# Combining the two maps of differential attention in parts of 512 keys, and ahead of the new pair's first maximum where two pairs join

## The reference, cut to what matters

```python
def diff_attention(q, k, v, lam, lam_init, g_sub, slopes):
    ...
    for i in range(S // Q_BLOCK):
        q0 = i * Q_BLOCK
        kend = q0 + Q_BLOCK
        s = jnp.einsum('bqhmd,bkhmd->bhmqk', q[:, q0:kend], k[:, :kend]).astype(jnp.float32) * scale
        ...
        s = jnp.where(allowed, s - slopes[:, None, None, None] * dist, NEG)
        p = jax.nn.softmax(s, axis=-1)
        a = p[:, :, 0] - lam * p[:, :, 1]
        outs.append(jnp.einsum('bhqk,bkhe->bqhe', a.astype(v.dtype), v[:, :kend]))
```

## Time and profile before

| | us |
|---|---|
| median of 3 runs | 2730.36 |
| lowest and highest | 2727.61, 2734.29 |
| the profiled execution's own time | 2732.85 |
| its span in the trace | 2730.8 |
| TensorE busy | 2586.2 (95% of the span) |
| VectorE busy | 1153.6 (42%) |
| ScalarE busy | 893.1 (33%) |
| GpSimd busy | 216.4 (8%) |
| share of TensorE in the chain that ended last | 75% |

### The profile page before, as it was taken

One profiled execution on the slowest core, in us unless ns is written; L12 is line 12 of the kernel. 1 busy time (PEld: TensorE's weight loads), 2 busy tenths in 40 slices (PEclk: granted clock), 3 DMA queues, 4 the chain that ended last, 5 costly groups with the idle time before them and its releaser, 6 DMA issues.

```text
span 2730.8 us, 33929 instructions
## 1 busy us (share of the span) xinstructions
PE 2586.2 (95%) x12825; PEld 2117.3 (78%) x12825; DVE 1153.6 (42%) x2309; ACT 893.1 (33%) x1572; POOL 216.4 (8%) x101
## 2 busy tenths in 40 slices
PE   7999999879999999999999999987899999999998
PEld 6778777668788888888878777765788888888886
DVE  5555566645322223223336546665542232232233
ACT  4554444433211212112236544444322121120222
POOL 1111111112000000000211111111110000000001
PEclk9999999999999999999999999999999999999999
DMA  5100010211111111111220000002111111111112
GB/s 174 55 24 24 16 32 24 62 39 45 46 47 46 54 46 46 54 46 52 94 86 24 24 24 24 24 24 68 47 39 54 46 46 54 46 46 54 45 47 77
DMA packets 219019, 131.42 MB, mean 48 GB/s; under 512 B 15222, under 2 KB 214432, under 8 KB 218664
## 3 DMA queue, kind: packets, MB, share of 16 engines
q1 hardware_dynamic: 213208, 114.38, 14.5%
q10 hardware_dynamic: 5712, 15.73, 1.5%
HBM read 117.47 MB, written 12.62 MB: 48 GB/s over the span
## 4 chain that ended last, share of the span: by engine, by line
PE 75%; issue 9%; DVE 8%; ACT 6%; DVEq 2%; DMA 0%; SPq 0%; ACTq 0%; POOL 0%; POOLq 0%
PE ps L1134 67%; DVE probs L912 2%; PE ps L1266 2%; PE ps L1286 2%; ACT probs L638 2%; ACT pt_hi L656 2%; PE ps L1213 1%; PE ps L1288 1%; DVEq L919 1%; DVE pt_lo L963 1%; DVE probs L940 1%; DVE neg_max L927 1%; ACT sink_exp L641 1%; DVE part L823 0%; PE ps L1115 0%
## 5 line engine op out<-in xcount | busy, mean ns | idle before, releaser
L1134 PE MATMUL ps<-wide_hi,w_hi 128*128 128x512 f32 x3016 | 960.1, 400 | 41.2 <-DVE v_parts L833 10.6
L1134 PE MATMUL ps<-wide_lo,w_hi 128*128 128x512 f32 x3016 | 939.7, 393 | 0.0
L1134 PE MATMUL ps<-wide_hi,w_lo 128*128 128x512 f32 x3016 | 937.6, 392 | 0.0
L1134 PEld LDWEIGHTS ps<-wide_hi,w_hi 128*128 128x128 f32 x3016 | 553.7, 190 | 176.7 <-issue 54.9
L1134 PEld LDWEIGHTS ps<-wide_hi,w_lo 128*128 128x128 f32 x3016 | 571.8, 190 | 122.6
L1134 PEld LDWEIGHTS ps<-wide_lo,w_hi 128*128 128x128 f32 x3016 | 571.5, 190 | 122.5
L638 ACT ACTIVATE probs<-probs,neg_max,slope 128x256 f32<-128x256 f32 (+7 forms) x256 | 202.4, 791 | 339.1 <-DVE neg_max L927 275.3
L714 ACT ACTIVATE w_hi<-w_raw 128x1024 fp32r<-128x1024 f32 x112 | 117.8, 1052 | 453.0 <-PE ps L1134 443.5
L963 DVE TENSOR_TENSOR pt_lo<-ps,pt_hi 128x512 fp32r<-128x512 f32 (+3 forms) x216 | 126.6, 586 | 262.1 <-ACT pt_hi L656 261.7
L718 ACT ACTIVATE ring<-ring 128x1024 f32<-128x1024 f32 x64 | 67.8, 1060 | 491.0 <-DVE ring L1069 491.0
L1089 DVE TENSOR_TENSOR xt<-ps,xt 128x1024 f32 x48 | 58.8, 1225 | 387.1 <-PE ps L1134 387.1
(11 more groups left out here) (139 smaller groups left out, 1836.5 us busy)
## 6 DMA issues: line engine op xcount, KB each, us to landing
w_raw<-in_w_up_dram SPq DMA_DIRECT2D x128, 256.0 KB, 3.0
w_raw<-in_w_down_dram SPq DMA_DIRECT2D x128, 256.0 KB, 3.0
w_raw<-in_w_in_dram SPq DMA_DIRECT2D x92, 256.0 KB, 3.3
x_saved<-xt ACTq DMA_DIRECT2D x16, 512.0 KB, 2.6
w_raw<-in_w_out_dram SPq DMA_DIRECT2D x32, 256.0 KB, 3.3
xt<-x_saved SPq DMA_DIRECT2D x16, 512.0 KB, 3.7
o_out<-cum_saved ACTq DMA_DIRECT2D x2, 2048.0 KB, 8.1
out_dram<-rows SPq DMA_DIRECT2D x4, 1024.0 KB, 5.7
```

Source lines behind the costliest of these rows:

```text
L1134: mm = T.matmul(ps[p][:, bass.ts(t, BANK)], w, h[:, bass.ts(t, BANK)], start=(start and n == 0), stop=(stop and n == 2))
```

## The change

The combination of a step is issued in parts of at most 512 keys, each with its own increment of `combined`, and the first half's transposes wait for the first part only; the second half's wait for the second. At the three joins between differential heads of a layer (steps 40, 48, 56), VectorE combines the last step of the old head before it takes the first maximum of the new head; at every other step the order stays. A function gives the count that a part has reached, and `NCOMB` (48) is the number of parts in a layer, where there were 32 increments.

```diff
     PHASE0 = [sum(phases(u) for u in range(t)) for t in range(NT + 1)]
     NPHASE = PHASE0[NT]
+    NCOMB = sum(phases(t) for t in range(FIRST_A * NQ, NT))
+
+    def combined_at(t, part):
+        return PHASE0[t] - PHASE0[FIRST_A * NQ] + part + 1
...
                     V.drain()
-                    V.scalar_tensor_tensor(out=probs[:, (2 * t) % 4, 0:width], in0=probs[:, (2 * t + 1) % 4, 0:width],
-                                           scalar=lam_ratio[:, c:c + 1], in1=probs[:, (2 * t) % 4, 0:width],
-                                           op0=ALU.mult, op1=ALU.add).then_inc(combined, 1)
+                    for k0 in range(0, width, BANK):
+                        k1 = min(width, k0 + BANK)
+                        V.scalar_tensor_tensor(out=probs[:, (2 * t) % 4, k0:k1], in0=probs[:, (2 * t + 1) % 4, k0:k1],
+                                               scalar=lam_ratio[:, c:c + 1], in1=probs[:, (2 * t) % 4, k0:k1],
+                                               op0=ALU.mult, op1=ALU.add).then_inc(combined, 1)
...
                     t = s.step
                     if s.first and t == 2 * NQ:
                         dve.wait_ge(cum_out, 16 * (l + 1))
-                    if s.first and t < NT:
+                    join = t % NQ == 0 and FIRST_A * NQ < t < NT
+                    if s.first and t < NT and not join:
                         biased_max(t, 0)
                     if s.first and t:
                         if ORDER[(t - 1) // NQ][0] == "A":
                             combine(t - 1)
                         else:
                             invert_sums(t - 1)
+                    if s.first and join:
+                        biased_max(t, 0)
...
                     elif ORDER[half.step // NQ][0] == "A":
-                        pe.wait_ge(combined, NQ * AH * l + half.step - NQ * FIRST_A + 1)
+                        pe.wait_ge(combined, NCOMB * l + combined_at(half.step, half.units[0][1] // 4))
```

## The result

The changed kernel takes 2738.9 us (median of 10 runs, 2737.0 to 2746.4), the kernel before in the same series 2733.2 (10 runs). The ratio is 1.0026, with a 95% interval of 1.0016 to 1.0037: slower by some 6 us, which is still within the 0.3% that the prediction called the same. The median lies above the predicted range of 2725 to 2737. The profiled execution took 2739.29 us, 6.4 more than the one before. Of the 7.9 us between the forecast of 2731.0 and the result, 2.8 lie in the kernel before: the forecast started from its median of three runs, 2730.36, and its median of ten is 2733.2. The change itself was forecast at +0.6 us and measured at +5.7.

What follows compares the result with a forecast made beforehand. TensorE, busy 95% of the span, bounds the kernel; its 28.3 us waiting for combinations was the ceiling. Terms of +0.98 us and -0.4 for the clock gave +0.6, so 2731.0 us from 2730.36; range 2725 to 2737.

Steps and rivals of the forecast that it cites:

- The question of which wait ends last: At each touched place, which wait holds TensorE last once its transposes no longer wait; the transposes' 28.3 us was the ceiling.
- the direct prices: A second part adds 0.14 us to VectorE, between 0.08 and 0.30, counting only ahead of a wait of TensorE.
- Join 40: Transposes start 1.27 us earlier, but this is stood out before the dense piece; each join at 40 and 48 costs 0.14.
- join 56: Two joins without a dense piece: the half's copy starts later behind the exponentials, +0.38 us each, +0.76 in all.
- five-block steps: Eight steps combining five blocks: +0.14 us in four, 0 in the third and last heads, sum +0.56.
- GpSimd comes between the parts: Rival: a GpSimd instruction of 2.40 us holds the second part; four such would be 9.6 us, 2741; chance 1%.
- -0.4 for two spells: TensorE's slow spells at step 48, one a layer: -0.2 us taken for each, with -1.5 left to the range.
- new ones to a rival: Rival: six new slow spells, at four joins and two wide steps, 1.5 us each, make 9: 2740; chance 6%.
- the 0.94 to 0.97: Test: the prediction is wrong if the mean clock of the two touched stretches leaves this range.
- The low part's wait on TensorE: TensorE's value products waiting for the half's low part, 27.6 us before: this wait should rise by about 2 us.
- VectorE's busy time: Over the whole kernel, it should rise by 4 to 7 us with 32 more combination instructions.
- the 0.53 kept at the end of the last head: At the last head's end, two places, the transposes' earlier start is kept whole: -1.06 us in all.

Runs made afterwards that it cites:

- e4: The kernel before with only the combination that runs in step 53 in two parts: 2741.6 us, ratio 1.0025.
- e10: As e4, with TensorE turning the identity 20 times while it waits at step 53: 2732.7 us, ratio 0.9992 to the kernel before.
- e3: The changed kernel, but with the combination that runs in step 53 left whole: 2736.8 us, ratio 1.0005 to the kernel before.
- e11: The kernel before with 14 dummy transposes ahead of the real ones at joins 40, 48 and 56: 2728.1 us, ratio 0.9969.

## Why the prediction was wrong

**What held.** The question of which wait ends last was right, and so were the direct prices. Step 37 to 38 took 0.13 us more and step 38 to 39 0.15 (layer 1: 0.13 and 0.13), predicted 0.14 each. Join 40 of layer 0 took 0.11 to 0.13 more, predicted 0.14, and the transposes, L837 and the dense piece each started within 0.02 us of where the working put them, counted from the first value product (375.23); only the standing before the dense piece was 1.27, not 1.45. At join 56 `L660` started right behind the exponentials and the value product came 0.30 later, predicted 0.38. The transposes' wait fell to 15.7, predicted 16.

**The step that failed** is the sentence on five-block steps: "In the third head GpSimd's work holds VectorE beyond it, and in the last TensorE isn't there yet: 0." I had seen that GpSimd ran there and took it as cover for the 0.14. It was the reverse: with a gap between two parts, the waiting GpSimd instruction came in between, and 0 became 1.13 us per layer, with a spell doubled in layer 0 and a new one in layer 1. In the last head, step 61, the same happened (2.92 us instead of 1.14) and the 0 held, as the sentence says, because TensorE comes for it only later: in layer 0 the parts end at 565.80 and the transposes start at 569.66. The mechanism even stands among the rivals, "GpSimd comes between the parts", with 1% and 2741, some 2 us from the result. That nearness is luck: it supposed four holds of 2.40 us, there were four of which two cost 1.13 each, and the clock and the kernel before's higher median made up the rest. It was argued away by one line alone: "No L510 of these stretches starts while a wide combination runs". That is true of the low parts of weights, L510. GpSimd's other instruction in the stretch, L515, was never looked up: at steps 53 and 61 it is queued behind another one, so that it is ready the moment the first part ends. The test was also wrong in kind: what matters isn't whether a GpSimd instruction runs during the whole combination, but whether one is queued then. At step 61 before, the division's record starts inside the whole combination (560.28) and lasts 2.48 us instead of 1.90: it was waiting.

The Trainium skill, "SBUF — State Buffer", section "SBUF: two separate sides", describes the lock as held for one whole instruction by whichever starts first; 2.68 us against 1.04 for the same two parts agrees. What follows for a split, that the port is given away in its middle, I did not draw from it.

**The clock** was the other mis-sized term. I took -0.4 for two spells that might shrink, and left new ones to a rival; measured, the clock took some 3 to 4 us more than before. In the profiled executions the change brought no net relief at the joins: of the four at steps 40 and 48 two carried a spell before (both 48s), and two after (40 and 48 of layer 1), although each standing was shorter. Standing of 1.27 us was followed by one at 1716.19, where the dense piece took 1.05 instead of 0.70; the same 1.27 in layer 0 was not. Of the granted clocks of 0.93 and 0.94 the first lies outside the 0.94 to 0.97 that the prediction asked for.

**The loss, summed:** 2.3 us directly at step 53, about 1 for the parts and joins as predicted, and some 2 to 3 by the clock, make the 5.7. The last is the remainder; the lost clock of the timed runs puts it at 2.7 to 4.4 (57.5 less 54.8 to 53.1). e4 and e10 show that step 53 alone can bring this much and more, but e3 loses as much clock without it, so where the change's spells come from is only in part shown.

**Two terms with the right sign for the wrong amount.** The low part's wait on TensorE rose by 5.1 us, not 2: at step 56 alone it rose by 1.58 a layer, since there it takes over what the transposes no longer wait. VectorE's busy time rose by 8.2 us, not 4 to 7: the parts held at steps 53 and 61 count as busy. And of the 0.53 kept at the end of the last head little is left. The transposes there start 598.35 - 596.88 = 1.47 us after the reciprocal, before 595.01 - 593.00 = 2.01, so 0.54 was won; but TensorE ran at half speed for longer, and the second dense piece behind came 10.02 us after the reciprocal (606.90), before 10.00 (603.00).

## What to carry to other kernels

Before an instruction is split, list everything that is queued on the engine with which it shares a port, by every line of that engine: each cut is a place at which the other may come in, for its whole length. Then ask at each such place which wait hides the delay: here it cost something at step 53 and nothing at step 61. A wait that changes its place costs what the clock makes of it: read the granted clock behind each piece of standing, not the standing alone. Where standing can't be removed, work of no use may hold the clock, as in e11, where 84 dummy transposes made the program 5 us faster.

## What the runs showed of the hardware

- A combination on VectorE and a division on GpSimd shut one another out by whole instructions: the two parts of a combination of 640 columns took 2.68 us with a queued GpSimd instruction of 1.9, and 1.04 without. Not every VectorE instruction is held: the second maxima of step 53 (L912) took their usual 0.47 us beside GpSimd's division, while `neg_max` behind them took 0.87 instead of 0.23.
- A spell at 1.2 GHz can follow standing of 1.27 us, and need not follow 1.90: join 40 and join 48 have the same work and the same 1.90 in the kernel before, and only the latter is followed by one. In the kernel before, step 53's standing of 1.41 us is followed by one in layer 0 and by none in layer 1.
- Between e4 and e10, and between the kernel before and e11, the only difference is what TensorE did in standing time whose end is the same. Where a spell was, behind step 53 and at join 48, the granted clock is then 1.00, and the medians differ by 8.9 us (e4 to e10) and 5.4 us (before to e11).
